# Splitting weights one chunk earlier on ScalarE than on VectorE, and a new order for gates, attention steps and the down projection

## The reference

```python
def residual_update(x, out, g_post, p_i, w_pp, w_pg):
    x = x + rms_norm(out, g_post)
    return x + (p_i @ w_pp) * jax.nn.sigmoid(x @ w_pg)

# first block, per layer
out = mixer(rms_norm(x, norm_pre[i]), w_in, w_out)      # q, k, v, g = h @ w_in; (attention * silu(g)) @ w_out
x = residual_update(x, out, norm_post[i], p[i], w_ple_proj[i], w_ple_gate[i])

# second block
proj = rms_norm(x, norm_mix_pre) @ w_in                 # q, k, v, gate_b, gate_c, hc
mix = concat([norm(diff_attention(q, k, v)), norm(gate_b * conv(gate_c * hc))]) @ w_out
x = x + rms_norm(mix, norm_mix_post)
hn = rms_norm(x, norm_ffn_pre)
f = (silu(hn @ w_gate) * (hn @ w_up)) @ w_down
x = x + rms_norm(f, norm_ffn_post)
```

## Time and profile before

| | |
|---|---|
| median of 3 runs | 2355.9 us (2354.93 to 2358.61) |
| profiled execution, its own time | 2369.29 us |
| its span in the trace | 2367.5 us |
| TensorE busy in the span | 2253.6 us (95%), 12428 matmuls |
| VectorE busy | 1402.3 us (59%) |
| ScalarE busy | 1162.2 us (49%) |
| mean granted clock of TensorE | 0.981 |
| HBM traffic | 389.50 MB read, 165 GB/s over the span |

### The profile page before, as it was taken

The page is one execution under the profiler, slowest core; times in us unless marked ns, Lnnn a source line. Parts: engine busy times, 40 slices in busy tenths (PEclk is TensorE's granted clock), DMA queues, the critical chain, the costliest instruction groups (busy, mean ns, idle before and its releaser), DMA issues.

```text
span 2367.5 us, 30040 instructions
## 1 busy us (share of the span) xinstructions
PE 2253.6 (95%) x12428; PEld 1925.5 (81%) x12428; DVE 1402.3 (59%) x1745; ACT 1162.2 (49%) x1532; POOL 8.3 (0%) x19
## 2 busy tenths in 40 slices
PE   7899999998999998979999999979999999999996
PEld 6688888886888886868888778868888888888885
DVE  5555555457686664467656766556565544556554
ACT  4455454555565554546544444544444444444453
POOL 0000000000000000000000000000000000000000
PEclk9999999999999999999999999989999999999998
DMA  6455656454666553445654445535666556566652
GB/s 217 147 159 166 181 160 183 136 184 132 193 180 176 149 150 111 143 157 181 189 167 155 142 130 169 178 116 163 185 187 188 187 187 187 178 196 178 191 174 98
DMA packets 220200, 393.57 MB, mean 166 GB/s; under 512 B 24889, under 2 KB 33730, under 8 KB 220064
## 3 DMA queue, kind: packets, MB, share of 16 engines
q1 hardware_dynamic: 218976, 389.40, 53.5%
q0 software_dynamic: 656, 1.41, 0.2%
q10 hardware_dynamic: 432, 0.85, 0.1%
HBM read 389.50 MB, written 2.11 MB: 165 GB/s over the span
## 4 chain that ended last, share of the span: by engine, by line
PE 78%; DVE 10%; ACT 6%; DMA 3%; issue 2%; DVEq 0%; SPq 0%; ACTq 0%
PE ps L737 77%; DVE WL L1176 4%; ACT WH L952 3%; DMA RAW<-in_w_out_a 1%; PE ps L741 1%; DVE TMP L1176 1%; DVE xT L1176 1%; ACT T L952 1%; ACT SQ L952 1%; DVE ACC L1176 1%; DVE TMPG L1176 0%; DMA RAW<-in_w_ple_proj 0%; DMA RAW<-in_w_ple_gate 0%; ACT gT L952 0%; DMA XN<-in_x 0%
## 5 line engine op out<-in xcount | busy, mean ns | idle before, releaser
L1176 DVE TENSOR_TENSOR WL<-RAW,WH 128x1024 fp32r<-128x1024 f32 x734 | 891.8, 1224 | 740.5 <-ACT WH L952 739.2
L737 PE MATMUL ps<-H,WH 128*128 128x512 f32 x3152 | 1129.0, 402 | 19.6 <-DVE H L1179 6.7
L952 ACT ACTIVATE WH<-RAW 128x1024 fp32r<-128x1024 f32 x734 | 767.4, 1055 | 664.4 <-PE ps L737 462.1
L737 PE MATMUL ps<-H,WL 128*128 128x256 f32 x3152 | 886.8, 281 | 0.0
L737 PEld LDWEIGHTS ps<-H,WH 128*128 128x128 f32 x3152 | 596.5, 189 | 167.7 <-issue 14.3
L737 PEld LDWEIGHTS ps<-H,WL 128*128 128x128 f32 x3152 | 599.3, 190 | 0.8
L737 PE MATMUL ps<-O,WH 128*128 128x512 f32 x1344 | 479.2, 400 | 26.8 <-DVE O L1176 19.8
L737 PE MATMUL ps<-O,WL 128*128 128x256 f32 x1344 | 377.5, 281 | 0.0
L737 PEld LDWEIGHTS ps<-O,WH 128*128 128x128 f32 x1344 | 254.5, 189 | 90.7 <-issue 30.2
L737 PEld LDWEIGHTS ps<-O,WL 128*128 128x128 f32 x1344 | 255.6, 190 | 0.1
L737 PE MATMUL ps<-ACTS,WH 128*128 128x512 f32 x704 | 249.2, 399 | 0.0
(11 more groups left out here) (201 smaller groups left out, 1468.9 us busy)
## 6 DMA issues: line engine op xcount, KB each, us to landing
RAW<-in_w_in_a SPq DMA_DIRECT2D x128, 512.0 KB, 3.8
RAW<-in_w_in SPq DMA_DIRECT2D x96, 512.0 KB, 3.7
RAW<-in_w_gate SPq DMA_DIRECT2D x88, 512.0 KB, 3.8
RAW<-in_w_up SPq DMA_DIRECT2D x88, 512.0 KB, 3.7
RAW<-in_w_down SPq DMA_DIRECT2D x88, 512.0 KB, 3.8
RAW<-in_w_ple_gate SPq DMA_DIRECT2D x64, 512.0 KB, 3.8
RAW<-in_w_in_b SPq DMA_DIRECT2D x40, 512.0 KB, 3.8
RAW<-in_w_out_a SPq DMA_DIRECT2D x32, 512.0 KB, 4.1
```

What stands on the lines that cost most here:

```text
L737: return e.matmul(o, l, r, start=start, stop=True, skip_group_check=True)
L952: return e.activation(o, i, f, **kw)
L1176: return e.tensor_tensor(o, x, y, op)
```

## The change

1. The split step falls into `split_hi` (ScalarE, as far ahead as before) and `split_lo` (VectorE, one chunk later in the list). SyncE's next transfer goes with `split_lo`.
2. A chunk's matmuls are put in two halves, with a turn of bg after each, so attention gets two turns per chunk. The attention tasks have more and shorter steps and more empty ones (None). In most chunks the order of the matmuls is k outer, tile inner.
3. The output projections have five groups, the last two with two tiles each. The residual units start with single tiles.
4. The pp groups put both parts of a tile in one place, with three matmuls of 256 columns (`one`), and need no addition. The first two gate groups take turns chunk by chunk, on eight banks (0 to 5, 6 and 7).
5. After the mixer, the first feed-forward gate group takes turns with half an up group, and the norm's factor (ffnpre) is computed from squares in bg and applied late, in place of a pair of ones matmuls in each residual unit.
6. The down projection uses the natural form. The addition of its two parts, the squares with their sums along a row (by ScalarE's accumulator) and the gain (GROW, one more transfer of 1 MB on GpSimd's queue) work on rows, so no transposes of the result are left, only those of x. The output goes in five transfers.
7. rstd: ScalarE's logarithm reads the bank directly, with scale and bias, and does not wait for VectorE's var.

```diff
 
     def splits(self, upto):
         while self.split <= min(upto, self.total - 1):
-            self.put("split", self.split)
+            self.put("split_hi", self.split)
             self.split += 1
-
-    def dense(self, g, banks=None):
...
+        g.chunks.append(i)
+        self.splits(i + AHEAD - 1)
+        for k in ks:
+            self.need((*g.x, k))
+        self.put("chunk", i, g.name, ci, ks, 0)
+        self.turn(self.bg)
+        self.put("chunk", i, g.name, ci, ks, 1)
+        self.turn(self.fg)
+        self.turn(self.bg)
+
...
-                    do("a_scores", p, bank=[6, 7]), do("a_exp", p), do("a_soft", p), None,
-                    do("a_cum", p), None,
+                    do("a_scores", p, bank=[6, 7]), do("a_exp", p), None, do("a_soft", p), None, None,
+                    do("a_cum", p), None, None,
                     do("a_pv", p, makes=[("pv", "A", p)]),
-                    (("g", "A", p // 2), do("gated", "A", p, makes=[("o0", h0), ("o0", h0 + 1)],
-                                            frees=[(6, ("ogate", "A", p)), (7, ("ogate", "A", p))])))
+                    (("g", "A", p // 2), do("gated", "A", p, frees=[(6, ("ogate", "A", p)), (7, ("ogate", "A", p))])),
+                    do("gated_low", "A", p, makes=[("o0", h0), ("o0", h0 + 1)]))
...
             def outproj(name, src, kts, xs, x, dst, norm):
-                for m in range(4):
-                    g = Group(f"{name}{m}", src, 512 * m, 4, kts, xs, x, dst=dst[:, 4 * m:4 * m + 4, :])
+                for n_, (t0, nt) in enumerate(OUTB):
+                    g = Group(f"{name}{n_}", src, P * t0, nt, kts, xs, x, per=8 // nt, dst=dst[:, t0:t0 + nt, :])
                     pl.dense(g)
                     pl.evict(g)
-                    for n_ in range(2):
-                        i = 2 * m + n_
...
                 pl.made |= {("ptile", l, 0), ("ptile", l, 1)}
-                pp(0)
-                rstd_now(norm)
-                pp(1)
...
+                early = pl.take(4)
+                late = [*pl.take(2), 6, 7]
+                pl.evict(pp(0, early[0:2]))
+                g = pp(1, early[2:4])
+                both(*rstd(norm))()
+                pl.evict(g)
+                units = residual(norm, pl.o_read, ("xs", l))
+                both(*units[0:2])()
+                pl.evict(pp(2, late[0:2]))
+                units[2]()
+                pl.evict(pp(3, late[2:4]))
+                pl.fg.append(task(*units[3:]))
+                gates = [Group(f"pg{l}_{m}", wpg, 512 * m, 4, K16, O, ("xs", l), dst=T[:, 4 * m:4 * m + 4, :],
+                               war=(("xres", norm, KD - 2),), slow=m < 2) for m in range(4)]
+
...
+                pl.begin(gates[0], early)
+                pl.begin(gates[1], late)
+                for _ in range(8):
+                    pl.feed(gates[0])
+                    pl.feed(gates[1])
+                gated(0)
+                gated(1)
+                pl.dense(gates[2], early)
+                gated(2)
+                pl.dense(gates[3], late)
+                gated(3)
+                pl.ring = early[0]
...
                 if part == 0:
                     for m in range(4):
-                        g = Group(f"dn0_{m}", wdn, 512 * m, 4, list(range(24)), ACTS, ("a", 0),
-                                  dst=T2[:, 4 * m:4 * m + 4, :])
+                        g = Group(f"dn0_{m}", wdn, 512 * m, 4, list(range(24)), ACTS, ("a", 0), natural=True,
+                                  dst=T2[:, :, 512 * m:512 * m + 512])
                         pl.dense(g)
                         pl.evict(g)
...
+            for m in range(4):
+                g = Group(f"dn1_{m}", wdn, 512 * m, 4, list(range(24, 44)), ACTS, ("a24",), natural=True, k0=24)
                 pl.dense(g)
-                pl.evict(g)
...
-                    for j, k in enumerate(ks):
+                    for j, k in list(enumerate(ks))[part * len(ks) // 2:(part + 1) * len(ks) // 2]:
...
+                js, ts_ = range(len(ks)), range(g.nt)
+                slow = not last and (g.slow or not first)
+                order = list(itertools.product(js, ts_)) if slow else [(j, t) for t in ts_ for j in js]
+                for j, t in order[part * len(order) // 2:(part + 1) * len(order) // 2]:
+                    b, k = g.banks[t // 2 if g.one else t], ks[j]
...
+                    g = groups[f"dn1_{m_}"]
+                    cols = slice(512 * m_, 512 * m_ + 512)
+                    dv.wait_ge(at("full", g.name, 0), at("ready", f"dn0_{m_}", 0))
+                    for t in range(2):
+                        tt(T2[:, t, cols], ps[:, g.banks[t], :], T2[:, t, cols], ALU.add).then_inc(
+                            *ev(evicted, ("dsum", m_, t), *([("free", g.name, 0)] if t else [])))
+                    dv.wait_ge(at("in", "grow"))
+                    for t in range(2):
+                        dv.wait_ge(at("dsq", m_, t), at("dsum", m_, t))
+                        tt(T2[:, t, cols], T2[:, t, cols], GROW[:, cols], ALU.mult).then_inc(
+                            *ev(added, ("dgain", m_, t)))
                 elif kind == "last_norm":
```

More of the change, by code:

```diff
@@ L100 @@
     tmp: bool = False
+    tmp0: int = 0
+    one: bool = False
+    slow: bool = False
+    late: bool = False
+    k0: int = 0
     war: tuple = ()
@@ new lines, in ordered @@
+            for n_ in range(4):
+                pl.feed(g0)
+                pl.feed(g0)
+                if n_ == 3:
+                    pl.evict(g0)
+                pl.feed(u0[0])
+            pl.evict(u0[0])
+            pl.dense(u0[1])
+            pl.evict(u0[1])
+            pl.need(("rs", "ffnpre"))
+            pl.put("late_scale", "fg0", "ffnpre", True)
+            for g in u0:
+                pl.put("late_scale", g.name, "ffnpre", False)
+            up(0, 0)
+            prev = ("up", 0)
@@ L741, in tr, with chunk @@
                 return e.transpose(o, i, idn)
[L743 removed]
+            def chunk(i, name, ci, ks, part):
                 g = groups[name]
@@ L751, in chunk @@
                     b = g.banks[0]
-                    if first:
+                    if first and part == 0:
                         for q in g.banks:
```

525 lines of the change are left out of this document (276 added, 249 removed).

## The result

The changed kernel took 2259.8 us in the median of 4 runs (2256.4 to 2262.8), beside 2357.3 for the kernel before in the same series: a ratio of 0.957, with a 95% interval of 0.953 to 0.962. Forecast were 2257, range 2230 to 2296. A second series gave 0.9569 (0.9538 to 0.9601). The profiled execution took 2257.75 us, its span is 2256.0. One slow run of the kernel before (4484.7 us, in the experiment that repeats it) is in no ratio.

What follows compares the result with a forecast made beforehand. TensorE was taken as the bound, with 114 us idle plus lower-clock losses. Gains of 83.5 (waits, clock), 9.2, 5.5 (transposes) and 9.8, less 5 and 4, gave 99 us: 2270 profiled, less 0.57%, 2257 us; range 2230 to 2296.

Steps and rivals of the forecast that it cites:

- Waits between ScalarE and VectorE in the residuals: Residuals of layers A and B: mutual wait goes, unit takes 3.30 us for 4.21; 14 and 13 us gained.
- The burst at the end of the gate pair: Both gate groups end together, additions and gupd rows delay low parts: 2.5 us new wait per layer, -5 us.
- the 4 I had set aside without a place: Allowance of 4 us lost to small waits of steps at new places, bounds 0 to 15.
- Attention B: End of attention B: two turns per chunk clear the backlog; 18 of 19.2 us gained, bounds 10 and 19.2.
- Convolution and C: Convolution beside attention C: only waits for high parts go; 6.5 of 14.1 us gained, bounds 0 and 14.1.
- Start of the mixer's output projection: Low parts of cnorm follow one unit later, so no wait within a unit: 4 of 4.8 us gained.
- Third residual: Third residual and first gate group: 7.3 us start, fewer chain waits and ones; 16 us gained, bounds 8 and 20.
- Down projection: Natural form takes 2.72 us per chunk for 2.83: 9.2 us gained over 88 chunks, bounds 0 and 9.5.
- Tail: After the last matmul, 12 us in place of 21.8: 9.8 us gained, bounds 8 and 11.
- Slots (1): Rival: later low parts free RAW slots later, each chunk takes 2.97 us; 2363 us, slower by 0.3%; chance 0.06.
- VectorE as the bound (2): Rival: VectorE bounds residual and convolution stretches, half the stall gains (42 us) stay out; 2299 us; chance 0.14.
- The pp triple: Three 256-column matmuls in pp, same 768 columns as before: costed at nothing, 0 to 12 us possible.

Runs made afterwards that it cites:

- the shift alone: Kernel before, with only the low part of each weight chunk one chunk later in VectorE's list than its high part in ScalarE's: 2337.3 us, ratio 0.985.
- two turns alone: Kernel before, with only the attention queue given two turns in place of one after each chunk: 2442.2 us, ratio 1.030.
- the second trace: Second profile of the changed kernel, run again with no edit: 2262.4 us in the median of 6 runs, span 2264.4.

## Why the prediction was right

The time came out 3 us from the forecast, and luck has a part in that. In the first pair of traces the change brought 111.5 us, in the second 101.8, not 99; some 4 us of the difference are the two values of a dense chunk. The reduction of 0.57%, from the profiled execution to the median of three runs, held for the kernel before in its first series alone: in the second its median (2368.7) lies at its profiled time, and the changed kernel's profiled executions (2257.8 and 2266.2) lie on either side of its medians (2259.8 and 2262.4). So 3 to 12 us too little gain met 13 us taken off at the end. That scaling was a step that no row carried.

Point by point:

- **Waits between ScalarE and VectorE in the residuals**: mechanism right, shown by the shift alone. In the changed trace a unit takes 3.07 us with no idle time ahead of the low part, and my 3.30 was high because three of the four rows start some 0.08 before the one ahead of them ends:

```profile
535.65 1.22 DVE L1246 TENSOR_TENSOR WL<-RAW,WH 128x1024 fp32r<-128x1024 f32 x1
...
538.72 1.22 DVE L1246 TENSOR_TENSOR WL<-RAW,WH 128x1024 fp32r<-128x1024 f32 x1
```

  Of the 16.5 us in the first residual the shift alone makes 7.5, the turns of the gates 2.4; the rest I put down to the way to the factor, covered by the pp groups, which no run took apart. In the stretches shown each loss came down to under 0.3 us where I kept 2.2.
- **The burst at the end of the gate pair (-5)** is the step that failed. The 32 gate chunks take 91.4 us in both layers, and 32 x 2.83 is 90.6. I had four additions (2.8) and four rows of gupd (2.8) pass before the next low part; the cover I named (5.65 us ahead) was evidently enough, though no run took it apart. The waits came elsewhere, in the latent stage (-5.1 and -4.3; a wait of 2.2 us for ACC and a short stretch at 1.2 GHz behind it), near the 4 I had set aside without a place.
- **Attention B**: 16.7 and 13.9 for 18. The backlog at this place is as I said: two turns alone bring 16.2 here. What the forecast left out is their price: the same run loses 88 us elsewhere. The changed kernel does not pay it, and I had not seen that anything was needed for that. It has the shift, more empty steps and half chunks beside the two turns; taking out the shift costs some 60 us, and the rest was not taken apart.
- **Convolution and C**: 10.0 and 8.0 for 6.5, with a wrong reason. "Only the waits for high parts go" predicts that the shift alone wins there; it wins nothing (170.5), nor do two turns alone (169.4), nor the changed kernel without its shift (170.4). Shift and the change's own attention steps together bring it to 158.5, and 4.9 of it needs the turn between the half chunks. Which of the other steps carries the rest was not tried.
- **Start of the mixer's output projection**: forecast +4, and it lost 2.6 (7.4 for 4.8; 0.8 by the second trace): TensorE waits 3.1 us for O, the low part of the last activations, and runs at 1.2 GHz for 6.8 us after. Low parts one unit later, my reason for the gain, did not keep TensorE from that wait. The sum of 20 for the mixer's end, the third residual and the first feed-forward part came out at 21.8 and 17.7; without the 4.3 us of the faster chunks both say some 17.5.
- **Third residual**: 7.3 us forecast from the last dense matmul, 8.6 measured (1494.67 to 1503.29; 15.6 before, counted alike). TensorE stands for 6.6 of them. Of the 1.3 that I missed, 0.6 lie at the start. ScalarE's copy of the last tile comes behind a high part of weights, and that one had waited for its transfer:

```profile
1494.37 1.06 ACT L1008 ACTIVATE WH<-RAW 128x1024 fp32r<-128x1024 f32 x1 [1.40 <-DMA RAW<-in_w_up]
1495.33 0.58 ACT L1008 ACTIVATE T<-ps 128x512 f32<-128x512 f32 x1
```

  The chain (start, us, what) that answers the earlier trace rows:

```profile
1495.94 0.70 DVE T L1246
...
1496.67 0.64 ACT SQ L1008
...
1497.35 1.15 PE ps L788 x4
...
1503.29 6.83 PE ps L788 x23
```

- **Down projection**: 2.83 to 2.72 us per chunk, 5.1 for 48 chunks, shown by itself in the kernel before. By the formula N / 2.4 + 2.5 ns in the Trainium skill, "TensorE: Matmul & The Clock Gate", section on the back-to-back issue gap, the gain would have been an estimated 0.9 us over 88 chunks, some 0.5 over 48. That section gives the formula for an isolated matmul and says that the spacing in a stream with weight loads goes by both, which my forecast left out; so the formula was no rule for this stream, and the runs don't agree with it: 5.06 were measured. Against chunks of 2.77 us the gain would be half of that, an estimate from the stretch above; the down projection had none of them in the traces. Transfers take longer to land (4.6 us for 3.8, at 200 GB/s; 4.7 with the shift alone too, in columns form), and ScalarE now waits for them and not for TensorE, but TensorE waits for none:

```profile
1791.46 1.06 ACT L1008 ACTIVATE WH<-RAW 128x1024 fp32r<-128x1024 f32 x1 [2.07 <-DMA RAW<-in_w_down]
1794.23 1.06 ACT L1008 ACTIVATE WH<-RAW 128x1024 fp32r<-128x1024 f32 x1 [1.71 <-DMA RAW<-in_w_down]
1795.88 1.06 ACT L1008 ACTIVATE WH<-RAW 128x1024 fp32r<-128x1024 f32 x1 [0.59 <-DMA RAW<-in_w_down]
```

- **Tail**: 12 forecast, 13.1 measured. The squares of the two rows of tokens run one after another (0.73 twice, I had 0.64 once), and the last transfer takes 3.8 us from VectorE's end for my 3.0. VectorE's end, to compare with the earlier trace rows:

```profile
2242.96 1.29 DVE L1246 TENSOR_TENSOR T<-ps,T 128x512 f32<-128x512 f32 x2 [6.07 <-PE ps L788]
2244.44 1.51 DVE L1246 TENSOR_TENSOR T<-T,GROW 128x512 f32<-128x512 f32 x2 [0.19 <-ACT TMP L1008]
...
2247.20 5.00 DVE L1249 SCALAR_TENSOR_TENSOR T<-T,RC,XNAT 128x1024 f32<-128x1024 f32 x5
```

- **Rivals.** Slots (1): high parts do wait for transfers in the down projection, as I named for its sign, but dense chunks take no more than 2.83 us (the second feed-forward part takes 226.1 us in both traces), so it was no cost there. Ahead of the third residual such a wait did reach TensorE, with the 0.6 us above. VectorE as the bound (2): hardly; with the gates in turn their stages come out at 91.4 us where 32 chunks need 90.6, and one after another they lose 2.4 and 3.7 us more. The pp triple costs little, if anything: the pp stage takes 12.6 us, four chunks of 2.83 (11.3) and 1.3 for all else.

## What to carry to other kernels

Where two engines work on the same item in turn and each has other work behind it in its list, put the second one's step one item later in the order: here that alone brought 33 us, and taking it out of the whole change cost some 60. An edit in a package can't be priced outside it: in one and the same stage the shift is worth 2.7 us with the old attention steps and 8.9 with the new ones, and two turns of attention per chunk are 72 us slower alone, though the changed kernel has them. To know which partner such an edit needs, run exactly the pair, and read the diff of the kernels, or their lists of steps, before you read the time. Don't scale a forecast from one profiled execution to a median by a factor seen on one kernel.

## What the runs showed of the hardware

On one chip the kernel before ran in two clusters 0.6% apart with the same mean clock, 0.980 to 0.984; the runs don't say why. A dense chunk at clock 1.00, with TensorE busy throughout, takes 2.77 or 2.83 us, in long runs of either: 221.8 and 226.1 us for the same 1282 matmuls in two executions of one kernel. No run shows what sets this, or whether the clusters come from it. The lower clock adds about half of the waits' time to them: span x 2 x (1 - clock) gives 90 us at 1.2 GHz before (0.981), some 32 after (0.993) and 132 with two turns alone (0.973), which is 45, 16 and 66 us of lost work beside 104, 28 and 148 us of waits.
